# Router logits with the rows moving in four column groups, the turn of the rows put amid the next second half, and GpSimd adding squares

## What is computed

```python
y = concatenate([rms(y_hy, gn), rms(y_lr, gn), rms(y_at, gn)])
x = _layer_norm(alpha * x + y @ w_out[l], ln_mix_g[l], ln_mix_b[l])
affinity = softmax(einsum("bsd,de->bse", x, router_w))   # 16 logits per token
gate, idx = top_k(swapaxes(affinity, 1, 2), 128)         # needs all tokens
```

## Time and profile before

| | |
|---|---|
| median of 3 runs | 1576.0 us (1574.22 to 1576.73) |
| the profiled execution | 1575.77 us, its span 1574.0 us |
| TensorE busy | 1485.1 us, 94% of the span |
| mix stage, tiles 2 to 6 | 14.55 us each |
| granted TensorE clock, whole span | 0.978 of full speed |

### The profile page before, as it was taken

How to read it: one execution, slowest core, us unless ns; L and a number is a source line. 1 busy time by engine, 2 the same in 40 slices (tenths; PEclk the granted TensorE clock), 3 DMA queues, 4 the chain that set the end, 5 groups by cost and what they waited for, 6 DMA issues and landing times.

```text
span 1574.0 us, 15700 instructions
## 1 busy us (share of the span) xinstructions
PE 1485.1 (94%) x5798; PEld 993.5 (63%) x5798; DVE 1001.3 (64%) x1014; ACT 721.3 (46%) x696; POOL 444.3 (28%) x225
## 2 busy tenths in 40 slices
PE   6999999999999999999999960999999999999997
PEld 3444487844344444555568850888888888888774
DVE  4533144442742564566535567799989989998896
ACT  3301000034522224455443441777777777777773
POOL 0031000000012004698973323033322223332204
PEclk9999999999999999999999985999999999999999
DMA  9311040015100000000123349799999999999994
GB/s 314 135 54 54 8 153 1 15 50 116 54 0 1 0 0 27 1 28 1 54 82 121 101 174 353 252 371 377 378 367 379 378 378 378 378 378 366 379 381 195
DMA packets 152885, 284.45 MB, mean 181 GB/s; under 512 B 25300, under 2 KB 35874, under 8 KB 152835
## 3 DMA queue, kind: packets, MB, share of 16 engines
q1 hardware_dynamic: 147219, 263.32, 47.1%
q0 software_dynamic: 4464, 16.25, 3.9%
q10 hardware_dynamic: 1152, 4.19, 0.7%
HBM read 259.10 MB, written 24.64 MB: 180 GB/s over the span
## 4 chain that ended last, share of the span: by engine, by line
PE 84%; DVE 6%; DMA 4%; ACT 2%; issue 2%; POOL 1%; SPq 0%; POOLq 0%; DVEq 0%; ACTq 0%
PE psum L1163 14%; PE psum L1621 9%; PE psum L1623 9%; PE psum L1622 9%; PE psum L1394 4%; PE psum L1256 4%; PE psum L1144 3%; DMA arena<-in_exp_w_down 3%; PE psum L1456 3%; PE psum L1364 3%; PE psum L1109 2%; PE psum L1532 2%; PE psum L1534 2%; PE psum L1533 2%; PE psum L1444 2%; PE psum L1272 2%
## 5 line engine op out<-in xcount | busy, mean ns | idle before, releaser
L2125 DVE TENSOR_TENSOR split_at<-arena,split_at 128x2048 fp32r<-128x2048 f32 x188 | 427.5, 2290 | 60.9 <-ACT split_at L1025 59.9
L1025 ACT ACTIVATE split_at<-arena 128x2048 fp32r<-128x2048 f32 x192 | 367.7, 1915 | 67.4 <-PE psum L1623 52.8
L1621 PE MATMUL psum<-split_at,split_at 128*128 128x512 f32 x768 | 305.9, 398 | 1.4 <-DVE split_at L2131 1.4
L1623 PE MATMUL psum<-split_at,split_at 128*128 128x512 f32 x768 | 300.2, 391 | 0.0
L1622 PE MATMUL psum<-split_at,split_at 128*128 128x512 f32 x768 | 299.4, 390 | 0.0
L1163 PE MATMUL psum<-arena 128*128 128x512 f32 x512 | 224.7, 594 | 1.4 <-DVE arena L1878 1.4
L1163 PEld LDWEIGHTS psum<-arena 128*128 128x128 f32 x512 | 96.1, 190 | 124.0 <-issue 123.9
L1623 PEld LDWEIGHTS psum<-split_at,split_at 128*128 128x128 f32 x768 | 144.4, 188 | 31.3
L1621 PEld LDWEIGHTS psum<-split_at,split_at 128*128 128x128 f32 x768 | 144.7, 188 | 29.7 <-DVE split_at L2131 1.8
L1622 PEld LDWEIGHTS psum<-split_at,split_at 128*128 128x128 f32 x768 | 144.9, 189 | 28.3
L600 POOL TENSOR_TENSOR arena<-arena 128x1024 f32<-128x1024 f32 x48 | 114.2, 2380 | 122.2 <-ACT arena L907 119.2
(11 more groups left out here) (302 smaller groups left out, 2202.4 us busy)
## 6 DMA issues: line engine op xcount, KB each, us to landing
arena<-in_exp_w_gate SPq DMA_DIRECT2D x64, 1024.0 KB, 14.4
arena<-in_exp_w_up SPq DMA_DIRECT2D x64, 1024.0 KB, 14.2
arena<-in_exp_w_down SPq DMA_DIRECT2D x64, 1024.0 KB, 14.4
arena<-in_w_in SPq DMA_DIRECT2D x9, 1024.0 KB, 8.5
arena<-in_x SPq DMA_DIRECT2D x8, 512.0 KB, 6.5
xhat_scratch<-arena SPq DMA_DIRECT2D x8, 512.0 KB, 9.9
arena<-in_w_out SPq DMA_DIRECT2D x8, 512.0 KB, 3.6
arena<-xhat_scratch SPq DMA_DIRECT2D x8, 512.0 KB, 4.9
```

What stands on the lines that cost most here:

```text
L1025: a(flat(wsplit[c % WS][0]), wraw[:, c], ACT.Copy).then_inc(s_whi, 1)
L1621: mm(bank(out_bank), src[0][:, k, :], whi[:, k % 4, :], start=(k == 0), stop=False)
L1623: ins = mm(bank(out_bank), src[1][:, k, :], whi[:, k % 4, :], start=False, stop=(k == KT - 1))
L2125: tt(flat(lo), wraw[:, c], flat(hi), ALU.subtract).then_inc(s_wlo, 1)
```

## The change

- Logits of tiles 0 to 6: for each of the 8 blocks the router's weights, widened with zeros to 32 columns, are stationary, and the 128 columns of `x1T` move. Block k goes to column group k mod 4, so that four groups of 32 PSUM partitions of bank 7 each hold a part (`logit_parts`, right behind the second half of the next tile; for tile 6 within the second half of tile 7). ScalarE copies the parts to SBUF (`logit_copy`), and one fp32 matmul with the copied parts stationary and a 0/1 matrix `lg_sum` moving adds the four parts and turns them (`logits_of_parts`, amid the first half of the tile after; for tile 6 behind the loop). Tile 7 keeps the old form.
- The turn of tile i-1 moves from ahead of tile i's squares to the middle of tile i's second half.
- GpSimd adds the four squared blocks in pairs for tiles 1 to 7 (`add_heads_squares`, two additions), so that TensorE sums them with one matmul instead of four.
- GpSimd clears `rw` once, SyncE waits for that, loads `rw` with a stride, and loads `lg_sum`.
- On ScalarE the copy of the turned rows goes behind the root and the exponential, followed by `logit_copy`; on VectorE the maximum goes ahead of the copy.

```diff
--- before.py
+++ after.py
@@ -219,7 +219,8 @@
         o_sq = mem(39888, 2, 4, P)
         xres, x1t = mem(28624, 2, D), mem(48080, 2, D)
         x1T = [mem(43984, D), mem(45008, D)]
-        rw = mem(52176, KT, NE)
+        rw, lg_part = mem(52176, KT, DR), mem(52432, 2, P)
+        lg_sum = mem(432, DR)
         accb = mem(46032, 2, D)
         affT = mem(9168, T // 2, p1=NE2)
 
@@ -278,6 +279,7 @@
         s_xh = s_x[0:2]
         s_res, s_mix, s_mixu, s_x1 = sem("residual"), sem("mix_psum"), sem("mix_read"), sem("x1_done")
         s_x1st, s_acst, s_acc = [sem(f"x1_stored{i}") for i in range(2)], [sem(f"acc_stored{i}") for i in range(2)], sem("acc_scaled")
+        s_lp, s_lc = sem("logit_parts"), sem("logit_parts_copied")
         s_x1p, s_x1ta, s_x1tv, s_lg = sem("x1_turned"), sem("x1T_act"), sem("x1T_dve"), sem("logits")
         s_rm, s_re, s_aff, s_afT = sem("router_max"), sem("router_exp"), sem("affinity"), sem("affinity_turned")
         s_topk, s_idxp, s_idxc = sem("topk_done"), sem("idx_turned"), sem("idx_ready")
@@ -506,7 +508,9 @@
             for dst, src in ((gmix, A["ln_mix_g"][0]), (bmix, A["ln_mix_b"][0])):
                 sp.dma_start(dst, src.partition_broadcast(P)).then_inc(s_gb, 16)
             sp.wait_ge(s_ov, N_OUT + 4)
-            sp.dma_start(rw, rows(A["router_w"][0])).then_inc(s_rw, 16)
+            sp.wait_ge(s_zero, 2)
+            sp.dma_start(rw[:, :, 0:NE], rows(A["router_w"][0])).then_inc(s_rw, 16)
+            sp.dma_start(lg_sum, A["c_rot"][:, P:P + DR]).then_inc(s_rw, 16)
 
             def load_chunk(e, c):
 
@@ -630,6 +634,13 @@
                     pool.wait_ge(s_mix, i - 1)
                 pool.tensor_tensor(ya_lo[:, i % 2], yT_at[:, :, P * i:P * i + P], ya_hi32[:, i % 2], ALU.subtract).then_inc(s_ol, 1)
 
+            def add_heads_squares(i):
+
+                pool.wait_ge(s_sq, SUMS + i + 1)
+                o = o_sq[:, i % 2]
+                link(pool.tensor_tensor(o[:, 0:2], o[:, 0:2], o[:, 2:4], ALU.add))
+                pool.tensor_tensor(o[:, 0], o[:, 0], o[:, 1], ALU.add).then_inc(s_sqa, 1)
+
             def residual(i):
 
                 res = xres[:, i % 2, :]
@@ -637,14 +648,18 @@
                 link(pool.tensor_tensor(res, res, gin, ALU.mult))
                 pool.tensor_tensor(res, res, bin_, ALU.add).then_inc(s_res, 1)
 
+            pool.wait_ge(s_qro, 2)
+            pool.memset(rw, 0.0).then_inc(s_zero, 1)
             pool.wait_ge(s_gb, 32)
             residual(0)
             heads_out_low(0)
             heads_out_low(1)
             residual(1)
+            add_heads_squares(1)
             for i in range(2, TT):
                 residual(i)
                 heads_out_low(i)
+                add_heads_squares(i)
 
             def gather_first(e):
 
@@ -987,6 +1002,13 @@
                     act.wait_ge(s_lg, i - 1)
                 a(x1T[i % 2][:, 0:HALF], bank(4), ACT.Copy).then_inc(s_x1ta, 1)
 
+            def logit_copy(i):
+
+                act.wait_ge(s_lp, i + 1)
+                if i >= 2:
+                    act.wait_ge(s_lg, i - 1)
+                a(lg_part[:, i % 2, :], bank(7)[:, P + P * (i % 2):2 * P + P * (i % 2)], ACT.Copy).then_inc(s_lc, 1)
+
             def mix_root(i):
 
                 act.wait_ge(s_st, TT + i + 1)
@@ -1002,11 +1024,12 @@
                 act.dma_start(acc_tok[:, i, :], accb[:, i % 2, :]).then_inc(s_acst[i % 2], 16)
 
             for i in range(TT):
-                if i:
-                    x1_copy(i - 1)
                 heads_root(i)
                 if i >= 2:
                     router_exp(i - 2)
+                if i:
+                    x1_copy(i - 1)
+                    logit_copy(i - 1)
                 if i + 2 < TT:
                     heads_out(i + 2)
                 mix_root(i)
@@ -1510,17 +1533,36 @@
                         ins = pe.transpose(bank(4 + b)[:, P * k:P * k + P], x1t[:, i % 2, HALF * b + P * k:HALF * b + P * k + P], ident)
                     ins.then_inc(s_x1p, 1)
 
+            def logit_parts(i):
+
+                if i == 0:
+                    pe.wait_ge(s_rw, 48 + 32)
+                if i >= 2:
+                    pe.wait_ge(s_lc, i - 1)
+                pe.wait_ge(s_rsd, ROOTS + i + 2)
+                pe.wait_ge(s_x1ta, i + 1)
+                pe.wait_ge(s_x1tv, i + 1)
+                for k in range(KT):
+                    p0 = DR * (k % 4)
+                    ins = mm(bank(7, 1, p0, p0 + DR)[:, P + P * (i % 2):2 * P + P * (i % 2)], rw[:, k, :], x1T[i % 2][:, P * k:P * k + P],
+                             start=(k < 4), stop=(k >= 4))
+                ins.then_inc(s_lp, 1)
+
+            def logits_of_parts(i):
+
+                pe.wait_ge(s_lc, i + 1)
+                if i:
+                    pe.wait_ge(s_re, i)
+                mm(bank(6)[:, NE * (i % 2):NE * (i % 2) + NE], lg_part[:, i % 2, :], lg_sum[:, 0:NE], start=True, stop=True).then_inc(s_lg, 1)
+
             def logits(i):
 
-                if i == 0:
-                    pe.wait_ge(s_rw, 48 + 16)
-                else:
-                    pe.wait_ge(s_re, i)
+                pe.wait_ge(s_re, i)
                 pe.wait_ge(s_x1ta, i + 1)
                 for k in range(KT):
                     if k == KT // 2:
                         pe.wait_ge(s_x1tv, i + 1)
-                    ins = mm(bank(6)[:, NE * (i % 2):NE * (i % 2) + NE], x1T[i % 2][:, P * k:P * k + P], rw[:, k, :], start=(k == 0), stop=(k == KT - 1))
+                    ins = mm(bank(6)[:, NE * (i % 2):NE * (i % 2) + NE], x1T[i % 2][:, P * k:P * k + P], rw[:, k, 0:NE], start=(k == 0), stop=(k == KT - 1))
                 ins.then_inc(s_lg, 1)
 
             pe.wait_ge(s_wol, KT)
@@ -1542,32 +1584,44 @@
                 if i:
                     pe.wait_ge(s_mxau, i)
                 for k in range(4):
+                    if i >= 2 and k == 1:
+                        logits_of_parts(i - 2)
                     ins = mix(0, k, y_hi[k // 2][:, k % 2, P * i:P * i + P], y_lo[k // 2][:, k % 2, P * i:P * i + P], k == 0, k == 3)
                 ins.then_inc(s_mxa, 1)
                 if i:
-                    x1_turn(i - 1)
-                pe.wait_ge(s_sq, SUMS + i + 1)
+                    pe.wait_ge(s_sqa, 7 + i)
+                else:
+                    pe.wait_ge(s_sq, SUMS + 1)
+                if i >= 2:
+                    pe.wait_ge(s_lc, i - 1)
                 if i == 0:
                     pe.wait_ge(s_ov, N_OUT + 4)
                 else:
                     pe.wait_ge(s_rsd, ROOTS + i)
-                for c in range(4):
-                    ins = mm(bank(7)[:, i:i + 1], o_sq[:, i % 2, c, :], ones[:, 0:1], start=(c == 0), stop=(c == 3))
+                for c in range(1 if i else 4):
+                    ins = mm(bank(7)[:, i:i + 1], o_sq[:, i % 2, c, :], ones[:, 0:1], start=(c == 0), stop=(c == (0 if i else 3)))
                 ins.then_inc(s_ssq, 1)
                 pe.wait_ge(s_ol, i + 1)
                 if i:
                     pe.wait_ge(s_mixu, i)
                 if i + 1 < TT:
                     for c in range(4):
+                        if i and c == 2:
+                            x1_turn(i - 1)
                         ins = mix(2, 4 + c, ya_hi[:, i % 2, c, :], ya_lo[:, i % 2, c, :], c == 0, c == 3)
                     ins.then_inc(s_mix, 1)
+                    if i:
+                        logit_parts(i - 1)
                 else:
                     for j in range(2):
                         for c in range(4):
+                            if j == 0 and c == 3:
+                                x1_turn(i - 1)
+                            if j and c == 2:
+                                logit_parts(i - 1)
                             ins = mix_half(2, j, 4 + c, ya_hi[:, i % 2, c, :], ya_lo[:, i % 2, c, :], c == 0, c == 3)
                         ins.then_inc(s_mix, 1)
-                if i:
-                    logits(i - 1)
+            logits_of_parts(TT - 2)
             x1_turn(TT - 1)
             pe.wait_ge(s_aff, TT - 1)
             for i in range(3):
@@ -2047,10 +2101,10 @@
                     v.wait_ge(s_acc, i - 1)
                     v.wait_ge(s_x1p, 2 * (i - 1))
                 stt(x, xres[:, b, :], ALPHA, bank(0, 2), ALU.mult, ALU.add).then_inc(s_mxau, 1)
+                if i >= 2:
+                    router_max(i - 2)
                 if i:
                     x1_copy(i - 1)
-                if i >= 2:
-                    router_max(i - 2)
                 v.wait_ge(s_rsd, ROOTS + i + 1)
                 v.reciprocal(ars[:, i:i + 1], asd[:, i:i + 1]).then_inc(s_on, 1)
                 if i >= 2:
```

## The result

The changed kernel takes **1577.9 us** in the median of 20 runs (1574.27 to 1583.58), for 1575.95 before (20 runs, 1574.02 to 1577.35). The ratio is 1.0015, with an interval of 1.0009 to 1.0021: slower by a little, where 7.6 us less was forecast and the range ended at 1572.6. The runs also spread more: 9.3 us between the extremes for 3.3 before. The profiled execution is one of 1579.67 us, 1.8 above the median, so what follows shows the loss somewhat larger than a usual run has it.

A forecast was written before the change was run, and what follows sets the result against it. TensorE's own work was taken as the bound, 14.55 us a tile. Savings over tiles 1 to 7 summed to 12.36 - 7X = 7.6 us at X = 0.68, giving a median of 1568.4 us, range 1565.2 to 1572.6.

The forecast's parts named there:

- What covers the rest: Step checking other engines' work in the loop: GpSimd's sum ready 0.4 us before TensorE wants it, so no cost.
- S: Time mark in the loop: the end of a tile's second half on TensorE, 895.08 us for tile 5.
- TensorE's own work bounds tiles 2 to 6: Main loop: TensorE busy for all 14.55 us of a tile, with nothing idle.
- a shift of the loop is kept whole: Behind the loop: what the loop saves shifts all that follows, counted at full worth.
- X: Time of the logits' parts on TensorE between second half and next first half; forecast 0.68 us with four groups overlapping.
- In-order: Rival at the logits' parts: strict program order, only neighbours overlap, X = 1.2, total 1572.0 us; chance 0.15.
- no-overlap: Rival at the logits' parts: column groups don't overlap, X = 1.96, total 1577.4 us; chance 0.04.
- bare-load: Rival at the logits' parts: short matmuls show their weight loads, X = 3.7, total 1589.7 us; chance 0.05.
- 12.71 + X: Length of a tile on TensorE after the change, in us, for 14.55 before.
- the forecast's own case: Loop total with X from 0.5 to 0.9, short GpSimd waits and cheaper short pairs: 1566 to 1570 us; chance 0.68.
- 12.22 + 0.68: Tile 1 on TensorE: 12.22 + X us for 15.38 before, with its turn's wait for VectorE gone.
- GpSimd holds the loop: Rival at GpSimd's additions: 2.0 us each makes the sum late, tiles 14.6, total 1575.1 us; chance 0.08.
- ScalarE late by 0.5: ScalarE behind a second half: copying the parts first makes the root and the finished rows 0.5 us late.

The follow-up runs named there:

- k1: Changed kernel without GpSimd's additions, TensorE summing the four squares again; 1570.93 us, ratio 0.9972 to the kernel before.
- k10: Changed kernel with VectorE's two normalising passes reading their second operand from PSUM, gain and bias left out; 1568.18 us, ratio 0.9947.
- k3: Changed kernel with TensorE summing four squares, while GpSimd adds constants into a spare tile that nobody awaits; 1571.22 us, ratio 0.9973.
- k6: Changed kernel with TensorE summing four squares and two unawaited GpSimd copies in place of the additions; 1571.53 us, ratio 0.9973.
- k4: Changed kernel with GpSimd's low part and additions ahead of the residual, once rows of tile i-2 are finished; 1566.4 us, ratio 0.9949.

## Why the prediction was wrong

**The step that failed** is "What covers the rest", GpSimd: "Ready at S + 17.8 + 0.5 + 1.3 = S + 19.6 ... So cost nothing, but the cover is thin". The additions were sized rightly when alone (0.73 and 0.46, as the slope gave 0.75 and 0.47). What was missing is that GpSimd's and VectorE's passes exclude each other. I had put the low part and the additions beside the normalising passes in time and never asked what they share. In the kernel before, the low part ended 0.08 to 0.64 us ahead of the pass in five tiles and ran 0.11 into it in the sixth, too little to show, and I read the constant 1.28 as a property of the pass, when it was one of the schedule. The shorter tile brought the low part onto the first pass (k1), and the additions onto the second. In tile 2 low part and first addition lost 0.97 and 0.98 that way, where 0.25 was to spare. A smaller part of the same step failed without the port: the spare of 0.4, or 0.25 in tile 2, was not there in every tile, and k10 still waits 1.1 in tile 7.

The Trainium skill, SBUF — State Buffer, section "SBUF: two separate sides", has the rule: the port pair that VectorE and GpSimd share is an exclusive lock, taken for the whole instruction by whichever starts first; on VectorE's side passes in a two-port mode take it, and passes with two SBUF inputs where the GpSimd pass reads SBUF. The traces agree for the normalising passes: turns (k3), GpSimd's copies as well as its additions (k6), none with the second operand in PSUM (k10). They differ a little on "whole": an overlap of 0.11 cost nothing, and a held-up instruction ends 0.14 to 0.27 us sooner than its full length behind the other. One SBUF operand isn't always a way out: L2084 reads one (beside a scalar for each partition, as the normalising passes have too) and took 2.35 instead of 0.23. By the rule that would be a two-port mode; no run here tests it. Read beforehand, the rule would have been the rival on the slower side.

**A second size was absent**: what an idle TensorE costs behind the wait. In tile 2, 2.15 us of idle were followed by 3.4 us at half the clock, 1.7 us more, and so were the 2.64 of tile 7; the waits of tiles 4 and 5 were not, and why is open. I had only looked at the clock behind the loop. The changed kernel's excess over a loop without waits is 4.0 + 1.8 + 3.1 in tiles 2, 4 and 5 and 4.5 in tile 7 (17.7 for 13.2 in k4), 13.4 us; waits of 9.1 and two slow stretches of 1.7 make 12.5 of it. That the waits depend on when a load lands, tile by tile, fits the wide spread of the runs; this was not tested by itself.

Point by point:
- *TensorE's own work bounds tiles 2 to 6, and a shift of the loop is kept whole*: right. In the profiles the loop from tile 1's start to the end of the last second half is 9.6 us shorter in k4, and the span is 9.6 us shorter (1564.4). In the changed kernel it is 3.8 us longer, and the span is 3.8 longer. That it comes out so evenly is in part luck: in k4 what lies ahead of tile 1 is 1.1 us shorter and what lies behind the loop 1.2 us longer.
- *X = 0.68*: 0.66, from 851.84 + 0.23 to 852.73. The row at 852.16 spans 0.64 for 16 instructions; less the last one's 0.27 that is 0.37, three distances of 0.12: they start in fours (in pairs it would be seven distances of 0.11, 0.75 in all). In-order, no-overlap and bare-load rivals are out: strict program order would take at least 9 slots, and 4 were taken.
- *12.71 + X = 13.39 a tile*: 13.09. The short pairs cost less than the mean of long rows, as the forecast's own case allowed.
- *Tile 1*: 12.22 + 0.68 = 12.90; 12.72 measured, its turn's wait gone.
- *The total*: 7.6 us for the loop without waits; k4 shows 9.2 to 9.6, mostly the 0.3 a tile.
- *GpSimd holds the loop*: this rival had the right place and, in the main, the wrong reason. It was priced by slow small copies, 2.0 for each, as if the price were GpSimd's own; measured were 1.7 and 0.46, and 1.0 more for the low part.
- *ScalarE late by 0.5*: about 0.3. In tile 3 the root starts at 855.53, S + 3.46, for S + 3.18 before.

## What to carry to other kernels

Before work is moved to an engine that "has room", list what it shares with the engine that has none: on GpSimd beside VectorE that is a port, and each VectorE pass with two SBUF operands that GpSimd's work meets adds up to nearly its own length to it (1.0 for a pass of 1.28 here), and the other way round. A cover of 0.4 us isn't a cover where two queues can meet; ask which passes fall onto each other once the period shortens, and place the side work where its engine waits for a load anyway (k4). A constant duration in a trace may be the schedule's, not the instruction's.

## What the runs showed of the hardware that I had not expected

- Four column groups of 32 with fp32 and 128 moving columns run fully side by side: 16 instructions take 0.66 us, going in and out included, where the old form took 1.70.
- A VectorE pass over 16 elements with one SBUF operand can take 2.35 us (L2084) for 0.23, when a GpSimd pass of 2.4 us has just begun.
- A VectorE pass that began 0.11 us before GpSimd's pass ended lost nothing (kernel before, tile 5).
- Waits of 2.15 and 2.64 us on TensorE in a loop that is otherwise full were each followed by 3.4 us at half the clock; one of 2.77 in the same loop was not.
